# A transformer stack in split fp32: the token operands begin at distances of their own from the 512-byte grid

## The reference

```python
def hybrid_layer(x, ...):                       # twice, weights of their own
    proj = x @ w_in                             # 2048 -> 4928 columns
    y_mla  = mla_mixer(...) * silu(g_mla)       # latent attention, 8 heads
    y_pool = pool_mixer(...) * silu(g_pool)
    y_conv = conv_mixer(...) * silu(g_conv)
    out = concatenate([y_mla, y_pool, y_conv]) @ w_out + b_out
    return layernorm(ALPHA * x + out, ln_g, ln_b)

def second_block(x, mem, ...):
    x = x + 0.5 * swiglu(rms_norm(x), w_gate, w_up, w_down)      # 2048 -> 5632 -> 2048
    proj = rms_norm(x) @ w_in                                    # queries, keys, values, forget logits
    mk, mv = rms_norm(mem) @ w_mem_k, rms_norm(mem) @ w_mem_v
    x = x + concatenate([fox, sliding_window, memory attention]) @ w_out
    x = x + 0.5 * swiglu(rms_norm(x), w_gate, w_up, w_down)
```

## Time and profile before

| | |
|---|---|
| median of 2 runs | 2531.15 us (2531.11 to 2531.19) |
| span of the profiled execution, first to last instruction | 2529.6 us |
| PE (matmuls) busy | 2513.3 us, 99% of the span, x12088 |
| PEld (weight loads) busy | 2107.5 us, 83%, x12088 |
| DVE busy | 1859.2 us, 73%, x2991 |
| ACT busy | 1323.1 us, 52%, x1893 |
| moved by DMA | 480.84 MB, mean 190 GB/s |
| share of TensorE's matmuls in the chain that ended last | 83% |

### The profile page before, as it was taken

The page is one execution under the profiler, slowest core; times in us unless marked ns, Lnnn a source line. Parts: engine busy times, 40 slices in busy tenths (PEclk is TensorE's granted clock), DMA queues, the critical chain, the costliest instruction groups (busy, mean ns, idle before and its releaser), DMA issues.

```text
span 2529.6 us, 33116 instructions
## 1 busy us (share of the span) xinstructions
PE 2513.3 (99%) x12088; PEld 2107.5 (83%) x12088; DVE 1859.2 (73%) x2991; ACT 1323.1 (52%) x1893; POOL 25.5 (1%) x24
## 2 busy tenths in 40 slices
PE   8999999999999999999999999999999999999999
PEld 6888888888888888888888887888888888888888
DVE  8787658787658777677777786678777767777766
ACT  6675565566566444444444455765544444444443
POOL 4000000000000000000000000000000000000000
PEclk9999999999999999999999999999999999999999
DMA  7555556455555555555555554444555555555554
GB/s 303 202 195 175 192 183 237 168 193 182 186 182 196 187 198 191 192 184 203 195 195 180 192 201 151 146 160 173 184 199 193 190 184 198 200 197 188 196 183 150
DMA packets 71231, 480.84 MB, mean 190 GB/s; under 512 B 8000, under 2 KB 10688, under 8 KB 17216
## 3 DMA queue, kind: packets, MB, share of 16 engines
q1 hardware_dynamic: 71104, 479.16, 53.4%
HBM read 475.72 MB, written 2.10 MB: 189 GB/s over the span
## 4 chain that ended last, share of the span: by engine, by line
PE 83%; DVE 1%; ACT 1%; issue 0%; ACTq 0%; DVEq 0%
PE acc L946 12%; PE acc L948 12%; PE acc L947 12%; PE score L946 10%; PE score L948 10%; PE score L947 10%; PE acc L932 8%; PE acc L936 4%; PE score L932 1%; PE score L1285 1%; DVE low L1787 0%; PE head_ps L1310 0%; PE score L936 0%; PE turn_ps L1294 0%; PE head_ps L1311 0%
## 5 line engine op out<-in xcount | busy, mean ns | idle before, releaser
L1787 DVE TENSOR_TENSOR low<-raw,high 128x1024 fp32r<-128x1024 f32 (+2 forms) x912 | 1079.5, 1189 | 460.2 <-ACT high L1374 451.5
L1374 ACT ACTIVATE high<-raw 128x1024 fp32r<-128x1024 f32 (+2 forms) x912 | 934.7, 1028 | 842.5 <-PE acc L948 435.9
L932 PE MATMUL acc<-xs,high 128*128 128x512 f32 x1184 | 393.4, 395 | 1.5 <-DVE xs L2331 1.2
L946 PE MATMUL acc<-high,xs 128*128 128x512 f32 x928 | 366.3, 395 | 0.3 <-DVE scale_a L1880 0.3
L948 PE MATMUL acc<-low,xs 128*128 128x512 f32 x928 | 361.6, 390 | 0.0
L947 PE MATMUL acc<-high,xs 128*128 128x512 f32 x928 | 361.1, 389 | 0.0
L936 PE MATMUL acc<-xs,low 128*128 128x256 f32 x1184 | 297.5, 278 | 0.0
L946 PE MATMUL score<-high,xs 128*128 128x512 f32 x736 | 286.4, 389 | 0.0
L948 PE MATMUL score<-low,xs 128*128 128x512 f32 x736 | 286.3, 389 | 0.0
L947 PE MATMUL score<-high,xs 128*128 128x512 f32 x736 | 286.3, 389 | 0.0
L932 PEld LDWEIGHTS acc<-xs,high 128*128 128x128 f32 x1184 | 219.2, 188 | 49.6 <-DVE xs L2331 1.9
(11 more groups left out here) (410 smaller groups left out, 3200.4 us busy)
## 6 DMA issues: line engine op xcount, KB each, us to landing
raw<-w_up_dram SPq DMA_DIRECT2D x176, 1024.0 KB, 4.8
raw<-w_in_dram SPq DMA_DIRECT2D x76, 1024.0 KB, 4.9
raw<-w_wide_dram SPq DMA_DIRECT2D x75, 1024.0 KB, 4.8
raw<-w_out_dram SPq DMA_DIRECT2D x32, 1024.0 KB, 4.8
raw<-w_heads_dram SPq DMA_DIRECT2D x20, 1024.0 KB, 4.8
raw<-w_mixout_dram SPq DMA_DIRECT2D x16, 1024.0 KB, 4.8
raw<-w_mem_dram SPq DMA_DIRECT2D x8, 1024.0 KB, 4.8
raw<-w_first_dram SPq DMA_DIRECT2D x8, 1024.0 KB, 4.8
```

The lines of the kernel that those rows point to most:

```text
L932: return eng.matmul(bank_, hi, moving, start=start, stop=False)
L946: eng.matmul(bank_, xh, hi, start=start, stop=False)
L1374: eng.activation(high[:, s % SPLIT, to:to + n * P], raw[:, s % RAW, at_:at_ + n * P], ACT.Copy).then_inc((highs_a, highs_b)[piece], 1)
L1787: eng.tensor_tensor(low[:, s % SPLIT, w], raw[:, s % RAW, at_:at_ + n * P], high[:, s % SPLIT, w].bitcast(F32), ALU.subtract).then_inc((lo ...
```

## The change

Each stage's token operand gets a start of its own, counted in words of 4 bytes. `begun` cuts the tiles out of an allocation that is a few words longer than before. `xs_of`, `hidden_of`, `mixs_of` and `in_mix` give the view for a norm, a region or a layer, and every place that named `xs`, `mixs`, `hidden`, `memh` or `mem_b` now asks them. 128 bytes are added behind the area of `memh`. No instruction is added, removed or reordered, and no wait changes.

```diff
-        xs = at("xs", [P, KT, 2 * S], F32R)
+        xs_all = at("xs", [P, KT * 2 * S + 16], F32R)
...
-        mixs = at("mixs", [P, KT, 2 * S], F32R, work)
+        mixs_all = at("mixs", [P, KT * 2 * S + 64], F32R, work)
...
-        hidden = at("hidden", [P, CT, 2 * S], F32R, work)
+        hidden_all = at("hidden", [P, CT * 2 * S + 16], F32R, work)
...
-        memh = at("memh", [P, KT // 2, 2 * S], F32R, memh_at)
-        mem_b = at("mem_b", [P, KT // 2, 2 * S], F32, memh_at)
+        memh_all = at("memh", [P, KT * S + 32], F32R, memh_at)
+        mem_all = at("mem_b", [P, KT * S + 32], F32, memh_at)
...
         assert cursor[0] == memh_at + 16 * KB
+        cursor[0] += 128
...
+        def begun(whole, words, tiles):
+            return whole[:, words:words + tiles * 2 * S].rearrange("p (k s) -> p k s", k=tiles)
+
+        def xs_of(norm):
+            return begun(xs_all, {"emb": 0, "ln0": 4, "ln1": 8, "mix": 2, "ffn2": 16}[norm], KT)
+
+        def hidden_of(r):
+            return begun(hidden_all, {"1": 4, "2": 12}[r.name[-2]], CT)
+
+        def mixs_of(n):
+            return begun(mixs_all, (64, 1, 0)[n], KT)
...
         def memory_tile(n):
-            return mem_b[:, n % 8, S:2 * S], memh[:, n % 8, :], p_("mem_g", n), mem_in[n // 8]
+            from_, to = (begun(a, (32, 6)[n // 8], KT // 2) for a in (mem_all, memh_all))
+            return from_[:, n % 8, S:2 * S], to[:, n % 8, :], p_("mem_g", n), mem_in[n // 8]
...
         def in_mix(r):
-            return memh if r.name[:3] == "mem" else mixs if r.name[:3] == "out" or r.name == "mixout" else xs
+            if r.name[:3] == "mem":
+                return begun(memh_all, (32, 6)[r.layer], KT // 2)
+            if r.name[:3] == "out" or r.name == "mixout":
+                return mixs_of(DEPTH if r.name == "mixout" else r.layer)
+            return xs_of("ln1" if r.name[:3] == "up1" else "ffn2" if r.name[:3] == "up2" else "mix" if r.kind == "natural"
+                         else ("emb", "ln0")[r.layer])
...
-                    eng.dma_start(mem_b[:, :, S:2 * S], t["mem"][:, 8 * r.layer:8 * r.layer + 8, :])\
+                    eng.dma_start(begun(mem_all, (32, 6)[r.layer], KT // 2)[:, :, S:2 * S], t["mem"][:, 8 * r.layer:8 * r.layer + 8, :])\
...
-                                last = product_natural(unit_bank(r, k, b), (xs if r.up else hidden)[:, row, :],
+                                last = product_natural(unit_bank(r, k, b), (in_mix(r) if r.up else hidden_of(r))[:, row, :],
...
-                        last = eng.matmul(head_ps[1][0:2 * FOX, :], wfs[:, kt, :], xs[:, kt, :], start=(kt == 0),
+                        last = eng.matmul(head_ps[1][0:2 * FOX, :], wfs[:, kt, :], xs_of("mix")[:, kt, :], start=(kt == 0),
...
-                    eng.tensor_tensor(mixs[:, w, S:2 * S], mix[:, w, :], mixs[:, w, 0:S].bitcast(F32), ALU.subtract)\
+                    eng.tensor_tensor(mixs_of(layer)[:, w, S:2 * S], mix[:, w, :], mixs_of(layer)[:, w, 0:S].bitcast(F32), ALU.subtract)\
```

More of the change, by code:

```diff
@@ L603, in hidden_pair @@
         def hidden_pair(r, k, i):
-            pairs = hidden[:, :, :].rearrange("p (u m) s -> p u m s", m=2)
+            pairs = hidden_of(r).rearrange("p (u m) s -> p u m s", m=2)
             return pairs[:, val(k // 4 - 1, 1, i), :, :]
@@ L1121, in slot @@
                                 piece_ready(int(b > 0))
-                            product_high(a, hl(b)[0], hidden[:, HALF * half + b, :], half == 0 and b == 0)
+                            product_high(a, hl(b)[0], hidden_of(r)[:, HALF * half + b, :], half == 0 and b == 0)
                         for b in range(first, end):
-                            last = product_low(a, hl(b)[1], hidden[:, HALF * half + b, :], half == 1 and b == HALF - 1)
+                            last = product_low(a, hl(b)[1], hidden_of(r)[:, HALF * half + b, :], half == 1 and b == HALF - 1)
                             if b in (r.pieces[0] - 1, HALF - 1):
@@ L1552, in layer_norm @@
                                 eng.wait_ge(embedded, KT // 2 * n + kt // 2 + 1)
-                            eng.activation(xs[:, kt, 0:S], x[:, kt, :], ACT.Copy, scale=p_("ffn1_g", kt)).then_inc(split_h, 1)
+                            eng.activation(xs_of(name)[:, kt, 0:S], x[:, kt, :], ACT.Copy, scale=p_("ffn1_g", kt)).then_inc(split_h, 1)
                         continue
                     eng.wait_ge(embedded, KT // 2 * n + j + 1)
-                    eng.activation(xs[:, 2 * j - 2:2 * j, 0:S], halves_of(affine[(j - 1) % 4]), ACT.Copy).then_inc(split_h, 2)
+                    eng.activation(xs_of(name)[:, 2 * j - 2:2 * j, 0:S], halves_of(affine[(j - 1) % 4]), ACT.Copy).then_inc(split_h, 2)
                     eng.wait_ge(embedded_v, KT // 2 * n + j + 1)
-                    eng.activation(xs[:, 2 * j:2 * j + 2, 0:S], halves_of(affine[j % 4]), ACT.Copy).then_inc(split_h, 2)
+                    eng.activation(xs_of(name)[:, 2 * j:2 * j + 2, 0:S], halves_of(affine[j % 4]), ACT.Copy).then_inc(split_h, 2)
                 if name != "emb":
@@ L1637, in do @@
                         eng.wait_ge(products, REG[source].g0)
-                    eng.activation(xs[:, kt, 0:S], x[:, kt, :], ACT.Copy, scale=p_(gain, kt)).then_inc(split_h, 1)
+                    eng.activation(xs_of(name)[:, kt, 0:S], x[:, kt, :], ACT.Copy, scale=p_(gain, kt)).then_inc(split_h, 1)
                 elif kind == "wide_square":
@@ L1724, in do @@
                         eng.wait_ge(head_out, HEADS * (layer + 1))
-                    eng.activation(mixs[:, 4 * c:4 * c + 4, 0:S], mix[:, 4 * c:4 * c + 4, :], ACT.Copy).then_inc(mix_h, 1)
+                    eng.activation(mixs_of(layer)[:, 4 * c:4 * c + 4, 0:S], mix[:, 4 * c:4 * c + 4, :], ACT.Copy).then_inc(mix_h, 1)
             def between(name):
@@ L1976, in split_low_of @@
                 eng.wait_ge(split_h, split_count(name, kt))
-                eng.scalar_tensor_tensor(out=xs[:, kt, S:2 * S], in0=x[:, kt, :], scalar=p_(gain, kt),
-                                         in1=xs[:, kt, 0:S].bitcast(F32), op0=ALU.mult, op1=ALU.subtract).then_inc(split_l, 1)
+                eng.scalar_tensor_tensor(out=xs_of(name)[:, kt, S:2 * S], in0=x[:, kt, :], scalar=p_(gain, kt),
+                                         in1=xs_of(name)[:, kt, 0:S].bitcast(F32), op0=ALU.mult, op1=ALU.subtract).then_inc(split_l, 1)
             def rotate(a, b, c, s_, out, out_b, count):
@@ L2330, in lows_of @@
                     w = slice(2 * i, 2 * i + 2)
-                    eng.tensor_tensor(xs[:, w, S:2 * S], halves_of(affine[i % 4]), xs[:, w, 0:S].bitcast(F32), ALU.subtract)\
+                    eng.tensor_tensor(xs_of(name)[:, w, S:2 * S], halves_of(affine[i % 4]), xs_of(name)[:, w, 0:S].bitcast(F32), ALU.subtract)\
                         .then_inc(split_l, 2)
```

## The result

The changed kernel takes 2578.87 us (median of 2 runs, 2578.58 to 2579.16) against 2531.15: ratio 1.0189, 95% interval 1.0159 to 1.0218. It is 47.7 us slower, outside the range of 2,480 to 2,560. The span grew by 47.2 us, from 2529.6 to 2576.8.

The account below looks back on a forecast made before the run. TensorE's matmul count times start-to-start distance was taken as the bound. Terms (a), (b) and (c) were each taken as 0, so the forecast stayed at 2,531 us, with a range of 2,480 to 2,560.

Parts of the forecast that it names:

- What bounds the kernel: TensorE's stream: number of matmuls times start-to-start distance; touched matmuls hold 150 us above their columns, 5.9% at most.
- (a): Token operands' starts against the weights, natural matmuls and pairs: cost taken as 0, between -133 and +42 us.
- The signs that I had named: In TensorE's trace: natural spacing going from 226.7 to 222 or 233 ns, or differing between up, wide and output stages.
- The page's rule: TensorE has two independent SBUF read ports, so loading weights takes nothing from the streaming read; (a) is exactly 0.
- Rival B: Distance costs: rows starting off a memory line need one more access before each exchange; +52 us, 2,583; chance 0.17.
- Rival C: The 64-byte shift behind xs makes distances other than written; forecast's time within a few us; forecast with C 0.62.
- (b): Entry of the pair stream: addresses may tip pairs between 347 and 353 ns; taken as 0, -2 to +10 us.
- (c): DVE and ACT writing and rereading moved token operands, plus the memory load; taken as 0, between 0 and +6 us.
- the 2% line: 2,480.5 us total, said to be passed from 5.5 ns saved per natural matmul and a like share on pairs.
- A: Rival: operands on the same 512-byte residue collide and distance lifts it; 2,465 if half, 2,398 if fully; chance 0.21.

Follow-up runs that it names:

- Runs 9 and 10: Kernel before with only 64 (up10/up11) and 16 (up20/up21) of 128 stationary columns loaded: 2544.79 us; the same with xs 64 bytes off the grid: 2552.80 us.
- Run 1: Kernel before with raw, high, low and all that lies behind them moved up by 64 bytes together: 2531.28 us, ratio 1.0000.
- run 6: Changed kernel with all written distances 0, keeping only the 64 extra bytes behind xs that move everything after it (the spill): 2551.59 us, ratio 1.0080.
- run 7: Second survey: changed kernel with the work area back on the grid and other token distances per stage, such as hidden 240 and 232 bytes: 2572.73 us.
- 13 and 16: Kernel before with high alone moved up 64 bytes: 2567.45 us; with high 64 bytes off in pair-order stages only, its ring slot 1 256 bytes off: 2533.08 us.

## Why the prediction was wrong

**What bounds the kernel** was right: no wait and no other engine moved, and the whole 47 us lie in TensorE's spacing, within the 7,932 natural matmuls and 1,592 pairs named, apart from 0.7 us on lats, which (a) names as moved by the 64 bytes but leaves out of the count.

**The step that failed is "I take 0" in part (a).** The price was 5.8 ns per natural matmul on average (46 us over 7,932): 6.6 in the up stages and wide2, 5.3 in wide1, 2.3 at 8 bytes. I had +5.3 as the upper end and took 0. The signs that I had named came: a natural spacing of 233, and another one in up than in wide. Each of the three reasons was a misreading:

- *"The excess is the same whether the row block is at 0 or at 512 bytes."* True, and no evidence: the period is 256 bytes, so these blocks never left the one good place. A constant over points that are all alike says nothing of the others.
- *"It stands at 18 ns where only 12 columns are loaded."* Runs 9 and 10 show that short loads have a longer spacing of their own, 230 ns on the grid. L1238 was probably slow in part for its 12 columns (no run tried 12), and the change moved its operands and hardly its spacing (232, 231). It could neither speak against a dependence on addresses nor price one; that its 5.3 ns came near the result was luck.
- *"It takes two values at the same addresses, so that it follows how the stream was entered rather than where the operands lie."* The one doesn't exclude the other: at one address stages do differ (228.3 and 226.7 ns at 240 bytes), and yet the address moved every natural stage by up to 6.6 ns.

**The page's rule.** The Trainium skill, page "TensorE: Matmul & The Clock Gate", section "Step-by-step: what each phase is for", lets a load take nothing from the streaming read. By it the change would cost 0. Run 1 against the change shows that this outcome doesn't hold for this pair of operands at full rate: the same reads cost 226.7 or 233.3 ns by their distance alone. Whether the load takes from the stream, or something else that the two reads share does, no run shows. The one agreement in the trace was with fp32 rows, which stream at half the rate; it said nothing of the full one.

**Rival B** had the sign and, by luck of its row, almost the size: +52 us against 47.7. Its mechanism (an extra access for a start off a line of the memory) is wrong, since run 1 starts off by 64 bytes and pays nothing, and multiples of 16, 32 and 64 pay the most. Its parts don't fit either: it has 42 us on natural matmuls and 10 on pairs, measured were 46 and 0.5. I gave it 0.17 and cut the range inside it. With 0 and +42 as the two ends and only one row near, the range should have held both.

**Rival C** had a real part: the spill alone costs 20.5 us (run 6), not "within a few us". I counted where it put each operand and didn't price it, although (a)'s upper end would have: 2,940 natural matmuls (660 x 3 on `hidden`, 256 x 3 on `mixs`, 192 on `memh`) x 5.3 = 16 us.

**(b) and (c)** were right: pairs moved by +0.5 us net, inside -2 to +10; DVE's subtraction stayed at 1,223 ns, the waits stayed. Two sums are a little off and change nothing: the 2% line is passed from about 5.1 ns per natural matmul with a like share on pairs (not 5.5), and the range leaves out 0.11 of A (not 0.10).

## What to carry to other kernels

When TensorE runs back to back in this format, the relative place of stationary and streamed operands is worth up to 3% of a matmul (6.6 of 226.7 ns), here 1.9% of the kernel. Where the tokens are the stationary operand, keep the two a multiple of 256 bytes apart, and when a buffer grows by a few bytes, look at what moves behind it. A row constant over many instructions bounds nothing outside the values that they cover: before taking 0, ask whether the trace contains a single case off them. Survey such a term by stages, each with a value of its own, in one run; the change itself turned out to be such a survey.

## What the runs showed of the hardware

- Natural order, 128 columns loaded, 512 streamed, clock 1.00: 226.7 ns in line, up to 234.1 out of line, period of 256 bytes (252 gives 226.7 on one operand and 233.3 on another); nothing lower in 20 kernels.
- Only relative place counts: 64 bytes on everything, 0.0% (0.9990 to 1.0009).
- The price isn't local: low alone off costs 5.3 ns per matmul, high alone 4.4 to 6.6, both 2.3. What the reads share and how it is arbitrated is open.
- Loading 64 or 16 columns instead of 128 lengthens the spacing from 226.7 to 230 ns (single runs).
- In pair order the best place is another: the loaded weights 64 bytes above both the tokens and the low part, 340.0 ns against 346.7 to 354.5; 192 does as well in layer 0. One address allows more than one steady spacing: 228.3 and 226.7 ns in run 7, 340.0 and 350.0 a pair on down21 in 13 and 16. The runs of one kernel differ too (2524.67 to 2528.86 us); that this has the same cause isn't shown.
- Behind a stall of TensorE of 2.65 us the granted clock was 0.50 for 2 us, and 116 matmuls ran in 25 us instead of 138.
